# Expert products with the rows stationary, and plain 32-bit down products, in a one-core streaming encoder step

## The reference

```python
def hier_moe(h, w_r1, b_r1, w_r2, b_r2, w_g, w_u, w_d):
    x = h.reshape(B * S, Dm)
    ...
    y = jnp.zeros((B * S, Dm), jnp.float32)
    for e in range(N_EXPERTS):                      # 32
        a = jax.nn.silu(x @ w_g[e]) * (x @ w_u[e])  # w_g, w_u: 1024 x 512
        y = y + gate[:, e:e + 1] * (a @ w_d[e])     # w_d: 512 x 1024
    return y.astype(h.dtype).reshape(B, S, Dm)
```

## Time and profile before

| what | value |
|---|---|
| median of 3 runs | 1157.56 us (1153.74 to 1158.6) |
| span of the profiled execution (first to last instruction) | 1142.0 us; no other time of it is given |
| mean granted TensorE clock | 0.910 |
| TensorE busy | 1083.6 us, 95% |
| TensorE weight loads | 882.8 us, 77% |
| VectorE busy | 402.0 us, 35% |
| ScalarE busy | 283.7 us, 25% |
| GpSimd busy | 84.8 us, 7% |
| moved by DMA | 264.56 MB, mean 232 GB/s |

### The profile page before, as it was taken

How to read it: one execution, slowest core, us unless ns; L and a number is a source line. 1 busy time by engine, 2 the same in 40 slices (tenths; PEclk the granted TensorE clock), 3 DMA queues, 4 the chain that set the end, 5 groups by cost and what they waited for, 6 DMA issues and landing times.

```text
span 1142.0 us, 16399 instructions
## 1 busy us (share of the span) xinstructions
PE 1083.6 (95%) x6668; PEld 882.8 (77%) x6668; DVE 402.0 (35%) x745; ACT 283.7 (25%) x485; POOL 84.8 (7%) x156
## 2 busy tenths in 40 slices
PE   6999999999999999989999999999999999999980
PEld 4666666456546655789999999999999999999970
DVE  1014440065312053314343525243433434252533
ACT  3013220023502133112222323131313222231321
POOL 2010000010100001400000000000000000000004
PEclk9996559965699998979999999999999999999995
DMA  8926003230204423278989899999989898988804
GB/s 238 385 96 258 1 1 111 74 120 1 74 1 161 171 74 139 91 260 321 361 340 352 337 353 340 350 354 342 370 331 365 336 357 336 355 339 324 290 11 147
DMA packets 54354, 264.56 MB, mean 232 GB/s; under 512 B 10648, under 2 KB 10672, under 8 KB 45712
## 3 DMA queue, kind: packets, MB, share of 16 engines
q1 hardware_dynamic: 46016, 236.18, 55.5%
q0 software_dynamic: 5600, 19.51, 5.5%
q10 hardware_dynamic: 2704, 8.39, 2.0%
HBM read 249.33 MB, written 16.58 MB: 233 GB/s over the span
## 4 chain that ended last, share of the span: by engine, by line
PE 91%; DVE 3%; DMA 3%; issue 1%; POOL 1%; ACT 1%; ACTq 0%; SPq 0%; POOLq 0%; DVEq 0%
PE pA L1151 39%; PE pS L1165 11%; PE pA L882 10%; PE pA L875 9%; PE pS L915 5%; PE pA L949 5%; PE pTr L1142 3%; PE pTr L930 2%; PE pA L857 2%; PE pTr L866 1%; PE pS L919 1%; DMA zone<-hn_d,idx_cur 1%; DMA zone<-y_d,slot 1%; POOL slot_d L592 1%; PE pA L1102 0%
## 5 line engine op out<-in xcount | busy, mean ns | idle before, releaser
L1151 PEld LDWEIGHTS pA<-zone,ring 128*128 128x128 f32 x4096 | 473.5, 194 | 4.6 <-issue 0.5
L1151 PE MATMUL pA<-zone,ring 128*128 128x64 f32 x4096 | 470.8, 276 | 0.0
L1487 DVE TENSOR_TENSOR zone<-zone,pS 64x1024 f32<-64x1024 f32 x32 | 38.8, 1212 | 349.2 <-ACT zone L774 349.2
L1482 DVE TENSOR_TENSOR w_lo<-ring,w_hi 128x1024 fp32r<-128x1024 f32 x128 | 150.5, 1218 | 19.8 <-ACT w_hi L761 19.8
L761 ACT ACTIVATE w_hi<-ring 128x1024 fp32r<-128x1024 f32 x128 | 127.7, 1046 | 30.5 <-DVE zone L1487 30.5
L774 ACT ACTIVATE zone<-pS 64x1024 f32<-64x1024 f32 x32 | 32.7, 1021 | 393.2 <-PE pS L1165 393.2
L882 PE MATMUL pA<-ring,hT 128*128 128x512 f32 (+1 forms) x240 | 106.3, 601 | 1.0 <-DVE hT L1236 1.0
L1165 PE MATMUL pS<-w_hi,a_split 128*128 128x512 f32 x256 | 104.1, 407 | 0.0
L1165 PE MATMUL pS<-w_lo,a_split 128*128 128x512 f32 x256 | 100.8, 394 | 0.0
L875 PE MATMUL pA<-hT,ring 128*128 128x320 f32 x320 | 91.1, 448 | 0.5 <-DVE hT L1236 0.5
L882 PEld LDWEIGHTS pA<-ring,hT 128*128 128x128 f32 (+1 forms) x240 | 41.3, 175 | 61.5 <-issue 60.9
(11 more groups left out here) (195 smaller groups left out, 732.4 us busy)
## 6 DMA issues: line engine op xcount, KB each, us to landing
ring<-in_w_exp_gate SPq DMA_DIRECT2D x32, 2048.0 KB, 10.6
ring<-in_w_exp_up SPq DMA_DIRECT2D x32, 2048.0 KB, 8.7
ring<-in_w_exp_down SPq DMA_DIRECT2D x32, 2048.0 KB, 13.9
ring<-in_w_in SPq DMA_DIRECT2D x6, 2048.0 KB, 21.4
y_d<-zone ACTq DMA_DIRECT2D x32, 256.0 KB, 5.0
ring<-in_w_out SPq DMA_DIRECT2D x2, 2048.0 KB, 18.4
ring<-in_w_ck SPq DMA_DIRECT2D x1, 2048.0 KB, 25.6
ring<-in_w_cv SPq DMA_DIRECT2D x1, 2048.0 KB, 7.7
```

Source lines behind the costliest of these rows:

```text
L1151: last = mm(pA[b][:, x * GW + f * SLOTS:x * GW + (f + 1) * SLOTS], w[:, c, f * P:(f + 1) * P], xeT[:, b, c, :], start=c == 0, stop=c == C - 1)
L1482: nv.tensor_tensor(w_lo[:, f, :], by_k(3 * b + 2, FC)[:, f, :], w_hi[:, f, :].bitcast(F32), ALU.subtract).then_inc(w_lo_ready, 1)
L1487: nv.tensor_tensor(ysb[:, b, :], ysb[:, b, :], pS[b][0:SLOTS, :], ALU.add).then_inc(y_summed, 1)
```

## The change

The operands of gate and up change sides: the 64 gathered rows (a 128 x 64 block of xeT) are stationary and 512 weight columns move, so that the output is 64 rows x 512. The sigmoid and the two multiplications work on 64 partitions x 512. TensorE then turns the activation rows by four transposes (hidden), and VectorE copies them to aT (hidden_in). The down product takes aT and the ring's weights as they are, in plain 32 bit; the splitting of weights and activations and their buffers go. Its two halves have one bank each, which ScalarE (left_rows) and VectorE (right_rows) copy out. All turned rows share one bank (xT_bank), the turned activations have the other. The down weights are laid out with 4 neighbouring rows a partition. The warming products in the loop go. A down slot of the ring is now awaited through y_ready. The final gains' buffer gfin lies in another place; declarations of semaphores and unchanged loops are cut below.

```diff
-        aT = zone[:, 3072:3072 + 2 * GW].rearrange("p (b f) -> p b f", b=2)
-        sg = zone[:, 3584:3584 + 2 * GW].rearrange("p (b f) -> p b f", b=2)
-        ysb = zone[0:SLOTS, 4096:6144].rearrange("p (b d) -> p b d", b=2)
+        aT = zone[:, 3072:3584].rearrange("p (b f s) -> p b f s", b=2, f=FC)
+        act_rows = zone[0:SLOTS, 3584:4608].rearrange("p (b f) -> p b f", b=2)
+        ysb = zone[0:SLOTS, 4608:6656].rearrange("p (b d) -> p b d", b=2)
...
-        w_hi = sb("w_hi", [P, FC, D], F32R)
-        w_lo = sb("w_lo", [P, FC, D], F32R)
-        a_split = sb("a_split", [P, 2, FC, 2, SLOTS], F32R)
...
+        up_bank = [pS[b][0:SLOTS, 0:512] for b in range(2)]
+        y_bank = [pS[b][0:SLOTS, 512:1024] for b in range(2)]
+        xT_bank, aT_bank = pTr[0], pTr[1]
...
                     sp.wait_ge(a_ready, a_done[RING + s])
-                elif n < 2:
-                    sp.wait_ge((gate_read, gu_ready)[n], r * NE + e - 1)
                 else:
-                    sp.wait_ge(w_lo_ready, (r * NE + e - 1) * FC)
+                    sp.wait_ge((gate_ready, up_ready, y_ready)[n], r * NE + e - 1)
...
-                if n < 2:
-                    dst, src = by_k(s), src.rearrange("(p c) n -> p c n", c=C)
-                else:
-                    dst, src = by_k(s, FC), src.rearrange("(c p) n -> p c n", p=P)
+                k = C if n < 2 else FC
+                dst, src = by_k(s, k), src.rearrange("(p c) n -> p c n", c=k)
                 sp.dma_start(dst, src).then_inc(w_in_s[s], 16)
...
-            def split(b, chunks):
-                for f in chunks:
-                    act.activation(w_hi[:, f, :], by_k(3 * b + 2, FC)[:, f, :], ACT.Copy).then_inc(w_hi_ready, 1)
             def sigmoid(n, b, first=False):
-                act.wait_ge(gu_ready, n + 1)
+                act.wait_ge(gate_ready, n + 1)
                 if not first:
-                    act.wait_ge(at_ready, n - 1)
-                act.activation(sg[:, b, :], pA[b][:, 0:GW], ACT.Sigmoid).then_inc(sig_ready, 1)
-            def lower_rows(n, b, first=False):
+                    act.wait_ge(ht_ready, n - 1)
+                act.activation(act_rows[:, b, :], pA[b][0:SLOTS, :], ACT.Sigmoid).then_inc(sig_ready, 1)
+            def left_rows(n, b, first=False):
                 act.wait_ge(y_ready, n + 1)
                 if not first:
                     act.wait_ge(y_stored[b], (n - b) * 8)
-                act.activation(ysb[:, b, :], pS[b][SLOTS:2 * SLOTS, :], ACT.Copy).then_inc(y_lower, 1)
+                act.activation(ysb[:, b, 0:512], y_bank[0], ACT.Copy).then_inc(y_left, 1)
             def rows_out(n, b, r, e):
-                act.wait_ge(y_summed, n + 1)
+                act.wait_ge(y_left, n + 1)
+                act.wait_ge(y_right, n + 1)
...
             def expert(r, e, b, first=False, first_out=False):
                 n = r * NE + e
-                lower_rows(n - 1, 1 - b, first_out)
-                act.wait_ge(w_in_s[3 * b + 2], (n - b) * 8 + 48)
-                split(b, (0,))
+                sigmoid(n, b, first)
+                left_rows(n - 1, 1 - b, first_out)
                 rows_out(n - 1, 1 - b, r, e - 1)
-                split(b, range(1, FC))
-                sigmoid(n, b, first)
             def experts(r):
                 n = r * NE
-                act.wait_ge(w_in_s[2], n * 8 + 48)
-                split(0, range(FC))
                 first = isinstance(r, int)
                 sigmoid(n, 0, first)
                 expert(r, 1, 1, first, first)
...
                 n += NE - 1
-                lower_rows(n, 1)
+                left_rows(n, 1)
                 rows_out(n, 1, r, NE - 1)
...
-            def transpose_rows(n, b):
+            def transpose_rows(n, b, first=False):
                 pe.wait_ge(xg_in[b], (n - b) * 8 + 16)
+                if not (first and b == 0):
+                    pe.wait_ge(xe_ready, n)
                 pe.nop().then_inc(pe_passed, 1)
                 src = xg[:, b, :].rearrange("s (p c) -> s c p", c=C)
                 for c in range(C):
-                    last = nc.tensor.transpose(pTr[b][:, c * SLOTS:(c + 1) * SLOTS], src[:, c, :], ident[0:SLOTS, 0:SLOTS])
+                    last = nc.tensor.transpose(xT_bank[:, c * SLOTS:(c + 1) * SLOTS], src[:, c, :], ident[0:SLOTS, 0:SLOTS])
                 last.then_inc(xt_ready, 1)
-            def product(n, b, x):
+            def product(n, b, x, bank, done):
                 pe.wait_ge(w_in_s[3 * b + x], (n - b) * 8 + 48)
                 w = by_k(3 * b + x)
+                for c in range(C):
+                    last = mm(bank, xeT[:, b, c, :], w[:, c, :], start=c == 0, stop=c == C - 1)
+                last.then_inc(done, 1)
+            def gate(n, b, first=False):
+                pe.wait_ge(xe_ready, n + 1)
+                if not first:
+                    pe.wait_ge(act_ready, n - 1)
+                product(n, b, 0, pA[b][0:SLOTS, :], gate_ready)
+            def up(n, b, first=False):
+                if not first:
+                    pe.wait_ge(act_ready, n - 1)
+                product(n, b, 1, up_bank[b], up_ready)
+            def hidden(n, b, first=False):
+                pe.wait_ge(act_ready, n + 1)
+                if not first:
+                    pe.wait_ge(at_ready, n)
+                pe.nop().then_inc(pe_passed, 1)
+                src = act_rows[:, b, :].rearrange("s (p f) -> s f p", f=FC)
                 for f in range(FC):
-                    for c in range(C):
-                        last = mm(pA[b][:, x * GW + f * SLOTS:x * GW + (f + 1) * SLOTS], w[:, c, f * P:(f + 1) * P],
-                                  xeT[:, b, c, :], start=c == 0, stop=c == C - 1)
-                last.then_inc(gu_ready if x else gate_read, 1)
+                    last = nc.tensor.transpose(aT_bank[:, f * SLOTS:(f + 1) * SLOTS], src[:, f, :], ident[0:SLOTS, 0:SLOTS])
+                last.then_inc(ht_ready, 1)
             def down(n, b, first=False):
                 pe.wait_ge(at_ready, n + 1)
+                pe.wait_ge(w_in_s[3 * b + 2], (n - b) * 8 + 48)
                 if not first:
-                    pe.wait_ge(y_summed, n - 1)
+                    pe.wait_ge(y_left, n)
+                    pe.wait_ge(y_right, n)
+                w = by_k(3 * b + 2, FC)
                 for f in range(FC):
-                    a = a_split[:, b, f, :, :].rearrange("p k s -> p (k s)")
-                    pe.wait_ge(w_lo_ready, n * FC + f + 1)
                     for half in range(2):
-                        for part in (w_hi, w_lo):
-                            last = mm(pS[b][0:2 * SLOTS, half * 512:(half + 1) * 512], a, part[:, f, half * 512:(half + 1) * 512],
-                                      start=f == 0 and part is w_hi, stop=f == FC - 1 and part is w_lo)
+                        last = mm(y_bank[half], aT[:, b, f, :], w[:, f, half * 512:(half + 1) * 512], start=f == 0, stop=f == FC - 1)
                 last.then_inc(y_ready, 1)
             def experts(r):
...
                 first = isinstance(r, int)
                 def expert(n, b, first=False):
-                    if not first:
-                        keep_warm(pA[b], 1, 256)
-                    pe.wait_ge(xe_ready, n + 1)
-                    product(n, b, 0)
+                    gate(n, b, first)
+                    hidden(n - 1, 1 - b, first)
+                    up(n, b, first)
                     down(n - 1, 1 - b, first)
-                    product(n, b, 1)
                     transpose_rows(n + 2, b)
-                pe.wait_ge(xe_ready, n + 1)
-                product(n, 0, 0)
-                product(n, 0, 1)
+                gate(n, 0, first)
+                up(n, 0, first)
                 transpose_rows(n + 2, 0)
-                for e in range(1, 4):
-                    expert(n + e, e % 2, first and e < 3)
+                expert(n + 1, 1, first)
+                expert(n + 2, 0)
+                expert(n + 3, 1)
...
-                keep_warm(pA[0], 3)
+                hidden(n + NE - 1, 1)
                 down(n + NE - 1, 1)
             keep_warm(pS[0], 5)
-            transpose_rows(0, 0)
-            transpose_rows(1, 1)
+            transpose_rows(0, 0, True)
+            transpose_rows(1, 1, True)
...
             def rows_in(n, b):
                 dve.wait_ge(xt_ready, n + 1)
-                nv.tensor_tensor(xeT[:, b, :, :], pTr[b][:, 0:C * SLOTS].rearrange("p (c s) -> p c s", c=C),
+                nv.tensor_tensor(xeT[:, b, :, :], xT_bank[:, 0:C * SLOTS].rearrange("p (c s) -> p c s", c=C),
                                  gcol[:, 4, :].unsqueeze(2).to_broadcast([P, C, SLOTS]), ALU.mult).then_inc(xe_ready, 1)
-            def activations(n, b, first=False):
-                dve.wait_ge(sig_ready, n + 1)
-                nv.tensor_tensor(sg[:, b, :], sg[:, b, :], pA[b][:, 0:GW], ALU.mult).then_inc(a_split_step, 1)
-                dve.wait_ge(a_split_step, n * 3 + 1)
```

(75 more changed lines are left out.)

1 line of the change is left out of this document (removed).

## The result

The changed kernel takes 1228.62 us (median of 4 runs, 1228.01 to 1230.02) against 1155.65 us before (4 runs, 1149.06 to 1158.60). The ratio is 1.065, with a 95% interval of 1.061 to 1.069: slower by 73 us. The forecast was 1238 us with a range of 1226 to 1256.

The account below looks back on a forecast made before the run. TensorE was taken as the bound, weight transfers close behind. Its period of 22.12 us against 19.56 gave +80.4 us, the end +0.3: span 1222.7, plus 15.6 around it, 1238 us; range 1226 to 1256.

Parts of the forecast that it names:

- A: Expert loop: plain 32-bit records as short as split ones, about 0.235 us, transfers bound the loop; about 1115 us; chance 3%.
- D: Expert loop: plain products cost what the removed ones did, 0.376 us a record, so no difference; chance 2%.
- Gate and up: TensorE per expert: 14.24 us of narrow records removed, 32 records of 0.429 us added, 13.73 us; gain 0.51.
- Down: TensorE per expert: 16 split records of 3.76 us become 16 plain ones of 6.86 us; loss 3.10.
- The warming product: TensorE per expert in the loop: the product goes, 0.54 us less, and nothing takes its place.
- the sum of the loop: TensorE per expert: 20.59 us of products plus 1.53 of turns, 22.12 against 19.56, +2.56 us.
- Waits and transfers: Expert loop: waits and transfers cost zero; burst landings at 8.7, 14.4 and 20.1 us, gate with eight us to spare.
- Rival B: Expert loop: the weight burst starves gate, landing later than 23.1 us; about 1269 us at 24.1; chance 6%.
- The beginning: First experts: TensorE's wait for the third gather and the slow clock from 490 to 506 us, about 8 us lost, both stay.
- rival C: First experts: the slow clock stretch goes, 8 us less, 1230, or another comes, 1246; no separate chance given.
- The end: From the last turn to the output row's last copy: 9.1 us against 8.8, +0.3; nothing moves behind it.
- The time around the span: Whole run: the 15.6 us between the profile's span and the median of the runs is kept, giving 1238 us.

Follow-up runs that it names:

- experiments 1: The kernel before with only the down product changed to plain 32 bit, without splitting of weights and activations: 1261.0 us, ratio 1.094.
- experiment 5: The changed kernel with SyncE's order of weight loads turned to gate n, up n, down n-1: 1229.26 us.
- experiments 2: The changed kernel with the split down product as before, gate and up with rows stationary: 1144.12 us, ratio 0.992.
- experiment 3: The kernel before without the warming product in the expert loop: 1142.43 us, ratio 0.988.
- experiment 6: The changed kernel with the turn of activation rows moved behind the turn of gathered rows: 1221.4 us, ratio 1.062 to the kernel before.
- experiment 7: The changed kernel with 12 memsets on GpSimd ahead of the third gather, to make TensorE idle there: 1233.28 us.
- experiment 4: The kernel before with four more warming products ahead of the first turn that waits for the third gather: 1149.94 us, ratio 0.997.
- experiment 9: The kernel before with five warming products instead of one ahead of expert 0's gate: 1138.35 us, ratio 0.988.

## Why the prediction was right, and where its numbers were off

**The bound and the mechanism.** Right. TensorE was and is the bound, all three products cost the same per record, and what ScalarE, VectorE and the transfers got back is worth nothing (experiments 1 and 5). Rivals A and D fell: the new records are 0.43 us apart in the loop too, where A wanted 0.235 and D 0.376. The Trainium skill, page "TensorE: Matmul & The Clock Gate", section "Wait — 56ns, not 53.3ns?", gives 215.7 ns from start to start of a warm matmul for N = 512. The split records, 0.23 us apart, come near it; the plain ones, 0.43 us apart, do not, and with two records a plain matmul takes 0.86 us, four times as long.

**Gate and up.** 13.73 us forecast, 7.01 + 6.92 = 13.93 measured: the products gain 0.31 us and not 0.51. With its turn it loses 0.41 against a loop without the warming product (experiments 2 and 3).

**Down.** 6.86 forecast, 6.96 measured, against 3.76. It is the whole loss: 3.00 of 2.98 us. The prediction counted three partial products in the split form; there are four, both parts of a_split against w_hi and w_lo, still in 16 records.

**The warming product.** I took 0.54 from the starts; taking it out gave 0.43. The start of a following product moves too when it goes.

**The turns and the passages.** This is what the sum of the loop lacked: 22.12 forecast, 22.54 measured, of which 0.15 are in gate (7.01 for 6.86), 0.11 in the turn of activations, 0.10 in down and 0.06 in up. I had no term for passages between products and turns, only 0.25 us as a bound for hand-overs. The difference is 0.42 x 31 = 13 us. Experiment 6 gave 0.29 of it back by taking one passage away; experiment 5 excludes the weights.

**Waits and transfers.** Right. TensorE doesn't idle in the loop, the burst lands within 0.2 us of the forecast for gate, 0.6 us later for down and 1.5 us earlier for up. Rival B has nothing for it (its 24.1 us for 20% less bandwidth should have been 20.1 / 0.8 = 25.1, which changes nothing). VectorE's copy of the turned activations took 0.42 us and not 0.29, still under up's 6.92.

**The beginning.** Wrong. I kept the wait for the third gather and the slow stretch of 8 us. Both are gone. Expert 0 started 1.9 us later and ran 0.7 longer, and the gather was issued 0.65 us earlier and landed after 4.1 us and not 8.7. Either would have done: with 8.7 us it would have landed at 488.3, just ahead of the turn at 488.42. That landing is no constant: the traces kept of six kernels here have 3.8 to 9.9 us for this gather. Experiment 7 shows that even with a wait of 3.1 us the clock would have come back after some 1.5 us of loss. This is half of rival C, -8 us.

**The end.** +0.3 forecast, +0.2 measured to the copy, and 1.6 more behind it, nearly all in the gathers of y_d's rows: the median from issue to landing is 7.2 us against 5.7. Why they were slower is not shown.

**The time around the span.** Wrong, and the largest error. I added 15.6 us, the distance of the profile's span from the median of the runs. A run takes 1.7 to 1.9 us more than its span. The profiled execution of the kernel before, with 1142.0 us and a clock of 0.910, was one of the faster group; the median, 1157.56, lies in the other one by its time. The changed kernel, whose runs agree within 2 us, has one group only.

Together: the span came out 5.6 above the forecast (+13 for the passages, -8 for the slow stretch, the rest at both ends), the time around it 13.9 below, and the profiled execution 1.4 above its median. That is the step from 1238 to 1228.6. That the span came out so near is in part luck, since the passages and the slow stretch err in opposite directions; and the largest error, the time around the span, was in no allowance of the range, which it used up almost to its lower end of 1226.

## What to carry to other kernels

Count records times the distance of their starts before changing sides of operands: here products of 64 narrow 32-bit records, 0.111 us apart, and of 16 wide ones, 0.43 us apart, came out nearly even, while giving up a split product nearly doubled its time (3.76 to 6.96 us). Work taken from engines beside the bound was worth nothing here, and the warming product inside a loop in which TensorE never idles was only cost. Where a kernel's runs fall into two groups, compare the profile's span and clock with them before its span is tied to their median.

## What the runs showed of the hardware

- TensorE was busy without a break for 41 us at a granted clock of 0.50 with 32-bit products of 64 moving columns (experiment 3), and the clock rose in the 512-column records that followed. After an idle time of 3.1 us a product of 512 moving columns was slow for about 3 us only (experiment 7).
- The clock fell to 0.50 within narrow products with TensorE busy for 3.5 us before, after an idle time of 0.25 us (experiment 4).
- A start at the low level made expert 0 of experiment 3 take 27.41 us and not 14.40. It is the likely cause of the two groups of the kernel before, some 10 us apart (3 of the 13 us would have gone into the wait for the gather); no trace of the slower group of that kernel itself was kept. Eight more warming records ahead of expert 0 removed the slower group (experiment 9: six runs within 1.8 us, where the kernel before had 18.5 beside it).
- A turn behind a 32-bit product of 512 columns starts its first weight load 0.95 us after the product's last load, where loads are 0.43 us apart inside; taking one such passage away saved 0.29 us (experiment 6).
- Three loads of 2 MB issued within 1 us landed after 9.3, 14.2 and 18.6 us, in their order.
